# The dense matmuls of two parts of the second feed-forward network, issued as two of 256 columns each

## What is computed

```python
def _swiglu(x, w_in, w_out):
    a, b = jnp.split(x @ w_in, 2, axis=-1)
    return (jax.nn.silu(a) * b) @ w_out
...
u = _modulate(_rmsnorm(h, norm1_g), sh1, sc1);  h = h + 0.5 * gt1 * _swiglu(u, ffn1_w_in, ffn1_w_out)
u = _modulate(_rmsnorm(h, norm2_g), sh2, sc2);  h = h + gt2 * _hybrid_mixer(u, ...)
u = _modulate(_rmsnorm(h, norm3_g), sh3, sc3);  h = h + 0.5 * gt3 * _swiglu(u, ffn2_w_in, ffn2_w_out)
return _rmsnorm(h, final_g)
```

## Time and profile before

| | |
|---|---|
| median of the two runs | 2134.32 us (2132.88 to 2135.76) |
| the profiled execution's own time | 2134.43 us |
| its span, first to last instruction | 2132.7 us |
| mean granted TensorE clock | 0.997 of full speed |
| DMA read and written | 539.70 MB, mean 253 GB/s |

### The profile page before, as it was taken

How to read it: one execution, slowest core, us unless ns; L and a number is a source line. 1 busy time by engine, 2 the same in 40 slices (tenths; PEclk the granted TensorE clock), 3 DMA queues, 4 the chain that set the end, 5 groups by cost and what they waited for, 6 DMA issues and landing times.

```text
span 2132.7 us, 23944 instructions
## 1 busy us (share of the span) xinstructions
PE 2089.8 (98%) x9531; PEld 1725.3 (81%) x9531; DVE 1511.5 (71%) x1705; ACT 1000.6 (47%) x1260; POOL 4.6 (0%) x22
## 2 busy tenths in 40 slices
PE   6999999999999999999999999999999999999998
PEld 5778788888888878888888887878888888888886
DVE  6887997888788888786555889577655454555456
ACT  4576433444344455446555644554443444434444
POOL 0000000000000000000000000000000000000000
PEclk9999999999999999999999999999999999999999
DMA  9998898997898868875444678658655555555554
GB/s 361 381 368 291 315 332 310 335 333 279 302 335 330 285 236 303 319 256 169 158 158 159 236 286 311 211 202 302 226 178 188 190 195 190 184 198 194 183 175 158
DMA packets 249135, 539.70 MB, mean 253 GB/s; under 512 B 11584, under 2 KB 13888, under 8 KB 248384
## 3 DMA queue, kind: packets, MB, share of 16 engines
q1 hardware_dynamic: 248640, 538.04, 71.6%
q10 hardware_dynamic: 384, 0.13, 0.0%
HBM read 536.03 MB, written 2.10 MB: 252 GB/s over the span
## 4 chain that ended last, share of the span: by engine, by line
PE 87%; DVE 2%; ACT 1%; issue 1%; DMA 0%; ACTq 0%; DVEq 0%
PE pa L618 14%; PE pb L618 14%; PE pa L621 14%; PE pb L621 14%; PE pa L620 14%; PE pb L620 14%; PE px L633 1%; DVE lo L1483 1%; ACT hi L1055 0%; DVE ada_acc L1572 0%; PE px L701 0%; PE pm L938 0%; PE px L946 0%; DMA raw<-in_w_in_dram 0%; DVE hid_lo L1643 0%
## 5 line engine op out<-in xcount | busy, mean ns | idle before, releaser
L1483 DVE TENSOR_TENSOR lo<-raw,hi 128x1024 fp32r<-128x1024 f32 (+1 forms) x744 | 882.1, 1194 | 543.9 <-ACT hi L1055 543.0
L1055 ACT CAST hi<-raw 128x1024 fp32r<-128x1024 f32 (+1 forms) x744 | 761.8, 1028 | 1003.8 <-PE pa L621 497.3
L618 PE MATMUL pa<-hi,act_hi 128*128 128x512 f32 (+1 forms) x1056 | 414.9, 393 | 7.2 <-DVE act_lo L1895 3.2
L621 PE MATMUL pa<-hi,act_lo 128*128 128x512 f32 (+1 forms) x1056 | 409.0, 387 | 0.0
L620 PE MATMUL pa<-lo,act_hi 128*128 128x512 f32 (+1 forms) x1056 | 408.7, 387 | 0.0
L618 PE MATMUL pb<-hi,act_hi 128*128 128x512 f32 x1024 | 403.0, 394 | 0.0
L621 PE MATMUL pb<-hi,act_lo 128*128 128x512 f32 x1024 | 398.8, 389 | 0.0
L620 PE MATMUL pb<-lo,act_hi 128*128 128x512 f32 x1024 | 398.5, 389 | 0.0
L1572 DVE SCALAR_TENSOR_TENSOR ada_acc<-ada_w,cond,ada_acc 128x1024 f32<-128x1024 f32 (+1 forms) x240 | 275.3, 1147 | 6.0
L618 PEld LDWEIGHTS pa<-hi,act_hi 128*128 128x128 f32 x1056 | 199.0, 188 | 51.8 <-DVE act_lo L1625 4.2
L621 PEld LDWEIGHTS pa<-hi,act_lo 128*128 128x128 f32 x1056 | 198.8, 188 | 41.2
(11 more groups left out here) (283 smaller groups left out, 1328.5 us busy)
## 6 DMA issues: line engine op xcount, KB each, us to landing
raw<-in_ffn_w_in_dram SPq DMA_DIRECT2D x176, 1024.0 KB, 4.9
ada_w<-in_w_ada_dram SPq DMA_DIRECT2D x224, 512.0 KB, 5.9
raw<-in_ffn_w_out_dram SPq DMA_DIRECT2D x64, 1024.0 KB, 5.1
raw<-in_w_in_dram SPq DMA_DIRECT2D x64, 1024.0 KB, 5.1
ada_s<-in_w_ada_dram SPq DMA_DIRECT2D x64, 512.0 KB, 9.6
raw<-in_ffn_w_out_dram SPq DMA_DIRECT2D x32, 768.0 KB, 4.5
raw<-in_w_out_dram SPq DMA_DIRECT2D x16, 1024.0 KB, 5.7
raw<-in_w_att_up_dram SPq DMA_DIRECT2D x8, 1024.0 KB, 5.1
```

Source lines behind the costliest of these rows:

```text
L618: pe.matmul(ps, a_hi[:, k0 + kk, tok], w_hi, start=start and kk == 0, stop=False, skip_group_check=on)
L621: mm = pe.matmul(ps, a_lo[:, k0 + kk, tok], w_hi, start=False, stop=stop and kk == n - 1, skip_group_check=on)
L1055: act.copy(hi[:, (2 * j + half) % 4, 0:n, 0:w], raw[:, j % RING, 2 * half:2 * half + n, 0:w])\
L1483: dve.tensor_tensor(lo[:, j % RING, s, 0:w], raw[:, j % RING, s, 0:w], hi[:, (2 * j + half) % 4, 0:n, 0:w].bitcast(F32), ALU.subtract)\
```

## The change

In the phases `ffn2_in1` and `ffn2_in2` each of the three matmuls of a product is issued as two of 256 columns: first the three for the left half of the bank's columns, then the three for the right half. The bytes read and written, the values, the waits and the semaphore at the end of a unit are the same. `start` is set on the first matmul of the left half alone. All other phases keep 512 columns (264 in `rest`).

```diff
             def unit(ph, i, j, half, k0, n, a_hi, a_lo, bank, start, stop, w=NC, on=False, tts=(0, 1)):
                 u = 2 * (ph.c0 + ph.per * i + j) + half
+                halved = ph in (plan["ffn2_in1"], plan["ffn2_in2"])
...
                         ps = bank[:, tt, 0:w]
+                        if halved:
+                            for c in (0, 1):
+                                cs = slice(c * (NC // 2), (c + 1) * (NC // 2))
+                                pe.matmul(ps[:, cs], a_hi[:, k0 + kk, tok], w_hi[:, cs],
+                                          start=start and kk == 0 and c == 0, stop=False, skip_group_check=True)
+                                pe.matmul(ps[:, cs], a_hi[:, k0 + kk, tok], w_lo[:, cs], start=False, stop=False,
+                                          skip_group_check=True)
+                                mm = pe.matmul(ps[:, cs], a_lo[:, k0 + kk, tok], w_hi[:, cs], start=False,
+                                               stop=stop and kk == n - 1, skip_group_check=True)
+                            continue
                         pe.matmul(ps, a_hi[:, k0 + kk, tok], w_hi, start=start and kk == 0, stop=False,
                                   skip_group_check=on)
```

## The result

The changed kernel takes 2151.44 us (median of two runs, 2151.05 to 2151.82) against 2134.32 us: +17.1 us, a ratio of 1.0081 with a 95% interval of 1.0064 to 1.0097. It is slower, as forecast, inside the range of 2131 to 2154 us, but by almost twice the 9.0 us of the forecast, and outside the +4 to +14 us of its favoured case. It lies at the time of rival A.

What follows compares the result with a forecast made beforehand. PE's matmul pace was taken to bound both phases; 1344 added matmuls at 6.7 ns a pair give +9.0 us, other terms nothing: 2134.3 + 9.0 = 2143.3 us, range 2131 to 2154 us.

Steps and rivals of the forecast that it cites:

- favoured case: In both phases each added matmul costs 8 to 12 ns beyond its columns: +4 to +14 us, chance 0.50.
- rival A: In both phases the wide matmul's fixed 13.3 ns stays whole, 120.0 ns each: +17.9 us, 2152.2 us, chance 0.25.
- What bounds the phases: `ffn2_in1` and `ffn2_in2` go at PE's own pace, so the difference arrives whole at the end.
- The count: In both phases 112 units of 12 dense matmuls: 1344 matmuls and 1344 weight loads added, no columns.
- term c: Each matmul's cost beyond streaming its columns, taken as 10.0 ns at 256 columns: 6.7 ns more a pair, +9.0 us.
- upper bound: A 256-column matmul takes no longer than the 120.0 ns of 264 columns: at most +17.9 us.
- The straight line through 264 and 512: Line through both measured widths, 0.430 ns a column, giving 116.6 ns for a matmul at 256 columns.
- The lower bound: Weight loads follow each other no faster than every 112.5 ns, so a pair costs at least 225.0 ns: -2.2 us.
- The turns and the borders: At five turns inside the two phases, the slow first triple costs 0.1 us at either width; costed at nothing.
- Rival B: PE's weight load sets the pace in both phases, second half free or better: 2132.1 to 2134.3 us, chance 0.18.
- Rival C: PE runs short of instructions, each queue packet costing a 0.9 us wait: about 2162 us, chance 0.05.
- Rival D: 256 columns fall out of fp32r's fast rate in both phases: +850 us, 2985 us, chance 0.02.

Runs made afterwards that it cites:

- run 1: Changed kernel with only `ffn2_in2` halved, `ffn2_in1` back at 512 columns: 2143.3 us against 2135.03 before the change, ratio 1.0042.
- run 10: Every dense 512-column matmul in all phases cut into 256+256, against the kernel before: 2238.7 us against 2133.77, ratio 1.0493.
- run 6: Both phases cut at 252+260 instead of the change's 256+256: 2145.74 us against 2133.77 before the change, ratio 1.0055.
- run 4: Changed kernel with one width per group (256, 252, 240; 504, 448, 384), columns omitted or repeated: 120.0 ns at 256, 115.6 at 252.
- run 5: Like the one-width-per-group run 4, with 248, 264, 272, 288, 320, 480 and 496 columns: 121.1 ns a matmul at 264.
- run 9: Changed kernel's two phases cut into four matmuls of 128 columns: 2431.14 us against 2132.84 before the change; 111.7 ns a matmul.
- run 7: Weight loads cut to 64 of 128 tokens in both phases, `ffn2_in2` at 512 columns: 113.3 ns at 256 columns, 230.0 at 512.
- run 2: Changed kernel with the halves inside each product, left then right: 2152.16 us, matmuls still 120.0 ns apart.
- run 8: Changed kernel with bfloat16 operands in `ffn2_in1` (113.4 ns at 256 columns, 225.0 at 512), loads of 32 or 96 tokens in `ffn2_in2` (117.8; 230 to 232).

## Why the prediction was right and where it was off

*What bounds the phases* was right. Nobody was waited for in them, and the cost arrived whole at the end: +17.8 us in the two phases, 17.1 us in the time. Runs 1 and 10 show it from both sides, additive where PE is never idle, and partly hidden where it is. The busy share of the loads near 100% was no sign of a new bound: it is the same in run 6, whose matmuls go by in 118 ns.

*The count* was right: 1344.

*The step that failed* is the term c: "I take c = 10.0 ns, since 264 is almost 256 and 512 is far off." It measures 13.3, so the sum is 17.9 and not 9.0 us. By the forecast's own sign, a pace of 116.7 ns in `ffn2_in1`, it was wrong: the pace is 120.0. The range held because it took in the upper bound of c. The straight line through 264 and 512 looked like a second witness, but it rests on the same two points and on the belief that c varies smoothly between them. The map of runs 4 and 5 shows that it does not: c is 11.1 at 264 columns (10.0 in `rest`), 13.3 at 256 and 10.6 at 252. The forecast's own second measurement, 13.3 at the width and place that were to be cut, was the better neighbour; it had been given a chance of 0.25. 252+260, a cut with widths to both sides of 256, comes at +8.9 ns a pair (c of 11.1), 248+264 at +8.1, both nearer to the 6.7 that were forecast than the +13.3 of the even cut.

*The upper bound* was right and tight: no more than the 120.0 ns of 264 columns, which is what 256 takes to the tenth. *The lower bound*, the pace of the loads, was not reached. As a floor it was 0.8 ns too high for fp32r (111.7 ns in run 9), and "no stream of single-use weights here goes faster" misread the trace: the eight transposes of a turn, each with a load of its own, are in the earlier trace rows itself at 1.03 us in all, and one is recorded at

```profile
L633 PE MATMUL px<-ident,buf_b x24: 272/272/273, 1725.9 to 1815.5; 128*128 128x128 f32 x24
```

so the last starts 0.76 us after the first, 109 ns a step. (These are plain float32, and each stands as one instruction.) At that pace a pair would have cost 218 ns and the bound would have been 11.7 us under the time of before, outside the range.

*The turns and the borders* at nothing: right. The second group of `ffn2_in1` takes 46.83 us from first start to last, 0.87 more than the first, which has no turn; before, a turn and the slow matmul behind it were about 0.9 us as well.

*Rival A* has the time, 2152.2 us forecast and 2151.44 measured. Its mechanism holds only in part: c is the same at 256 and 512 columns, but no fixed cost of a matmul, since the widths between them show 10.6 to 16.7 ns. That the two agree is luck as far as these runs tell. *Rival B* fell: the pace is 8 ns above that of the loads in run 9. It still is not without a part: run 7 gains 6.7 ns by halving the load. (The 6.7 ns of c at which B was said to decide is where a pair breaks even; the load of 112.5 ns would set the pace under 5.8.) *Rival C*: 10 packets more, as counted, and no idle time as issue. *Rival D*: no width down to 64 leaves the fast rate.

What stays open is what c is made of. It does not hang on the order of the products or on PSUM neighbours (run 2), hardly on where a slice begins (run 4), only in part on the number format (run 8), and on the load's length in a way that changes its sign between 256 and 512 columns and is not even monotone (runs 7 and 8). And it is gone at the 1.2 GHz level (run 10), and down to some 3 ns where plain float32 streams at half rate: it shows in full only where a column passes every 0.42 ns. The even values, 120.0 and 226.7 ns against the ragged ones of 252 or 448 columns, look like load and stream falling into step, but that is a guess and no run here tests it.

## What to carry to other kernels

Where the trace shows PE as the bound with nothing in front of it, count matmuls and not only columns: in fp32r at the full clock each one, with its own weight load, costs 10 to 17 ns beyond its columns here, so the widest moving operand wins, and a stream of matmuls of 128 columns takes 112 ns each, twice the time of its columns. A cost that is read at a neighbouring size is a bound, not a value; if the sum hangs on 3 ns of it, keep both measured values as cases of equal weight. And a longer matmul is paid in full only where PE never waits: the same cut cost 10.2 us in a phase without waits and 4.6 us in one that had 5 us of them.

## What the runs showed that was not expected

504 columns take as long as 512 (226.7 ns), and 256 almost as long as 264 (120.0 and 121.1), while 252 takes 115.6: leaving out the last 8 columns of a full matmul saves nothing, and leaving out 4 of 256 saves 4.4 ns. At the 1.2 GHz level the cost beyond the columns is gone: cutting a matmul in two was free there. A weight load of 64 columns makes a matmul of 256 columns 6.7 ns faster than one of 128 columns does, a load of 32 only 2.2 ns, and both make a matmul of 512 columns 3 to 5 ns slower. bfloat16 matmuls (every second element read) with their own loads, recorded at half the fp32r load's duration, are only 1.7 ns faster at 512 columns (225.0 against 226.7) and 6.7 ns at 256.
